# Stick-breaking stage: GpSimd multiplies the first 512 columns of each unit's weights, VectorE the rest

## What is computed

```python
for blk in range(S // SB_BLOCK):                 # 4 blocks of 128 tokens
    z = einsum('bthd,bshd->bhts', q[:, t0:t1], k[:, :t1]) * scale
    before = s_idx < t_idx
    log_beta = log_sigmoid(z)
    log_1m_beta = where(before, log_sigmoid(-z), 0.0)
    tail = cumsum(log_1m_beta, axis=3, reverse=True) - log_1m_beta
    a = where(before, exp(log_beta + tail), 0.0)
    outs.append(einsum('bhts,bshd->bthd', a, v[:, :t1]))
```

## Time and profile before

| | us |
|---|---|
| median of three runs | 2065.1 (2062.42 to 2067.36) |
| profiled execution, whole | 2061.98 |
| its span | 2060.2 |
| TensorE busy | 2018.9 (98%) |
| VectorE busy | 1097.0 (53%) |
| ScalarE busy | 737.7 (36%) |
| GpSimd busy | 227.6 (11%) |

### The profile page before, as it was taken

The page is one execution under the profiler, slowest core; times in us unless marked ns, Lnnn a source line. Parts: engine busy times, 40 slices in busy tenths (PEclk is TensorE's granted clock), DMA queues, the critical chain, the costliest instruction groups (busy, mean ns, idle before and its releaser), DMA issues.

```text
span 2060.2 us, 27336 instructions
## 1 busy us (share of the span) xinstructions
PE 2018.9 (98%) x11013; PEld 1679.3 (82%) x11013; DVE 1097.0 (53%) x1411; ACT 737.7 (36%) x1043; POOL 227.6 (11%) x205
## 2 busy tenths in 40 slices
PE   8999999999999999989999999999999999999998
PEld 7887888888888888868888888888888778888886
DVE  5764765645354453492735445466775435444453
ACT  6444544422122332584412222332673332222221
POOL 4000222300000130002200000322102010000002
PEclk9999999999999999999999999999999999999999
DMA  6231002132222322103222222234213112222221
GB/s 255 82 105 59 23 23 82 62 115 90 102 102 83 121 82 102 42 2 123 82 102 102 82 102 102 103 124 152 82 68 117 62 62 90 95 102 102 94 90 62
DMA packets 28332, 186.91 MB, mean 91 GB/s; under 512 B 3536, under 2 KB 3664, under 8 KB 6480
## 3 DMA queue, kind: packets, MB, share of 16 engines
q1 hardware_dynamic: 25200, 173.48, 23.5%
q0 software_dynamic: 2320, 11.01, 1.5%
q10 hardware_dynamic: 720, 1.11, 0.2%
HBM read 181.39 MB, written 2.10 MB: 89 GB/s over the span
## 4 chain that ended last, share of the span: by engine, by line
PE 90%; DVE 6%; ACT 2%; DMA 1%; issue 1%; POOL 0%; ACTq 0%; DVEq 0%; SPq 0%; POOLq 0%
PE PS L590 88%; DVE Y L2254 1%; DVE KEEP L2638 1%; DVE Y L2638 1%; DVE WL L2254 1%; DMA STG<-weights 1%; DVE Y L2251 1%; ACT WH L1533 1%; DMA MX<-mem_t 0%; PE PS L817 0%; DVE HL L2254 0%; PE PS L619 0%; POOL SQA L474 0%; DVE SQ L2254 0%; ACT SQ L1533 0%
## 5 line engine op out<-in xcount | busy, mean ns | idle before, releaser
L590 PE MATMUL PS<-HH,WH 128*128 128x512 f32 x1544 | 607.6, 394 | 1.0 <-DVE HL L2254 0.8
L590 PE MATMUL PS<-HH,WL 128*128 128x512 f32 x1544 | 601.5, 390 | 0.0
L590 PE MATMUL PS<-HL,WH 128*128 128x512 f32 x1544 | 590.9, 389 | 0.0
L1533 ACT ACTIVATE WH<-STG 128x2048 fp32r<-128x2048 f32 (+2 forms) x168 | 307.2, 1829 | 517.5 <-PE PS L590 516.5
L2254 DVE TENSOR_TENSOR WL<-STG,WH 128x2048 fp32r<-128x2048 f32 (+1 forms) x160 | 358.4, 2240 | 250.1 <-ACT WH L1533 249.9
L590 PEld LDWEIGHTS PS<-HH,WH 128*128 128x128 f32 x1544 | 290.2, 188 | 65.5 <-issue 5.2
L590 PEld LDWEIGHTS PS<-HH,WL 128*128 128x128 f32 x1544 | 290.0, 188 | 60.3
L590 PEld LDWEIGHTS PS<-HL,WH 128*128 128x128 f32 x1544 | 290.2, 188 | 59.9 <-issue 0.7
L590 PE MATMUL PS<-UPH,WH 128*128 128x512 f32 x832 | 324.2, 390 | 1.4 <-DVE UPL L2251 1.4
L590 PE MATMUL PS<-UPH,WL 128*128 128x512 f32 x832 | 323.7, 389 | 0.0
L590 PE MATMUL PS<-UPL,WH 128*128 128x512 f32 x832 | 323.7, 389 | 0.0
(11 more groups left out here) (319 smaller groups left out, 1992.2 us busy)
## 6 DMA issues: line engine op xcount, KB each, us to landing
STG<-weights SPq DMA_DIRECT2D x159, 1024.0 KB, 4.8
KEY_STG<-weights POOLq DMA_DIRECT2D x4, 1024.0 KB, 6.0
XT<-x_t SPq DMA_DIRECT2D x2, 1024.0 KB, 10.3
KEY_X<-mem_t POOLq DMA_DIRECT2D x2, 1024.0 KB, 5.3
out_t<-Y SPq DMA_DIRECT2D x8, 256.0 KB, 2.0
STG<-weights SPq DMA_DIRECT2D x4, 256.0 KB, 6.0
MX<-mem_t ACTq DMA_DIRECT2D x4, 256.0 KB, 7.8
CON<-consts SPq DMA_DIRECT2D x1, 1024.0 KB, 7.1
```

Of the source, the lines that this page charges most:

```text
L590: return pe.matmul(o, l, r, start=start, stop=stop, **kw)
L1533: return act.activation(o, i, f, **kw)
```

## The change

The products of the first 512 columns of all 12 units move from VectorE's stream to GpSimd's. There they stand between the sum of B.in and load_keys(2). They count a new semaphore, sb_wp. TensorE waits for it before the first group of transposes, and ScalarE waits for both before it overwrites KEEP. VectorE keeps the product of columns 512 to 1280.

```diff
@@ gpsimd
             split_lo(R0["B.qk"] + 1)
             sum_squares("B.in")
+            for n in range(12):
+                a, b = SB_PARTS[0]
+                pool.wait_ge(sems["sb_beta"], n + 1)
+                pool.wait_ge(sems["sb_scan"], 4 * n + 2)
+                pool.tensor_tensor(BETA[n % 2][:, a:b], BETA[n % 2][:, a:b], KEEP[n % 2][:, a + 1:b + 1], ALU.mult)\
+                    .then_inc(sems["sb_wp"], 1)
             load_keys(2)
@@ tensor: turn(n)
                     for h in range(2):
-                        pe.wait_ge(sems["sb_w"], 2 * n + h + 1)
+                        pe.wait_ge(sems["sb_w" if h else "sb_wp"], n + 1)
@@ scalar: stick_parts(n)
                 if n >= 2:
-                    act.wait_ge(sems["sb_w"], 2 * n - 2)
+                    act.wait_ge(sems["sb_w"], n - 1)
+                    act.wait_ge(sems["sb_wp"], n - 1)
@@ vector: weights(n)
                     dve.wait_ge(sems["sb_beta"], n + 1)
-                    for h in range(2):
-                        a, b = SB_PARTS[h]
-                        dve.wait_ge(sems["sb_scan"], 4 * n + 2 * h + 2)
-                        tt(BETA[e][:, a:b], BETA[e][:, a:b], KEEP[e][:, a + 1:b + 1], ALU.mult)\
-                            .then_inc(sems["sb_w"], 1)
+                    a, b = SB_PARTS[1]
+                    dve.wait_ge(sems["sb_scan"], 4 * n + 4)
+                    tt(BETA[e][:, a:b], BETA[e][:, a:b], KEEP[e][:, a + 1:b + 1], ALU.mult).then_inc(sems["sb_w"], 1)
```

More of the change, by code:

```diff
@@ L111 @@
 out_ready ow par_in gains_in pool_mm pool_s pool_z qd rcnt_in rk rope_cos rope_done rope_in
-df_b rows_in rows_tr rq rs rsc rv sb_z sb_half sb_keep sb_beta sb_first sb_scan sb_w sb_t sb_at sb_o
+df_b rows_in rows_tr rq rs rsc rv sb_z sb_half sb_keep sb_beta sb_first sb_scan sb_w sb_wp sb_t sb_at sb_o
 lv_t sc_act sc_dve sc_k sc_ws spread sig silu sq sqa sqrt ss st tile t1 gated0 u_mm u_sb uh ul vn vr_mm xf zeroed vrow vtr w_sb
```

## The result

The changed kernel is slower: median 2068.0 us against 2063.0 for the kernel before, run beside it, 20 runs each. The medians differ by 5.0; the ratio is 1.0021 (95% interval 1.0015 to 1.0027), that is +4.3 us (3.1 to 5.6), and the text goes by it. One run of the kernel before took 3417.19 and is no part of the ratio. Forecast was +5.3, slower by over 0.2%, and a median of 2070.5; the kernel before had 2065.1 in its first three runs, from which that was counted, and 2063.0 in all 20.

The account below looks back on a forecast made before the run. VectorE was taken to bound the stick-breaking stage. Added 12.4 less removed 7.1 gave +5.3 us on the median of 2065.1: 2070.4, rounded up to 2070.5; range 2065.5 to 2075.5.

Parts of the forecast that it names:

- VectorE carries the stage, TensorE and ScalarE have room: Stick-breaking stage: VectorE gapless for 56.3 us, 4.63 a unit; TensorE busy 4.18 and ScalarE 4.01 of that.
- Removed, 12 x 0.59 = 7.1: Twelve 512-column products leave VectorE, 0.59 us each, all on the chain: 7.1 us saved.
- Added, 12 x 1.03 = 12.4: Each of twelve GpSimd products costs VectorE 1.03 us through turns over SBUF: 12.4 us, bounds 0 to 15.5.
- The row that gave 1.03: Two VectorE operations with two SBUF inputs took 2.44 us beside one GpSimd product, 1.41 without: 1.03 lost.
- The scan is held like a product: VectorE's scan, reading SBUF twice, was taken to wait for GpSimd as products do; no row showed it.
- Where it lands: GpSimd's turn delays the fourth scan in odd units or the 768-column product in even ones, by about 1.03 us.
- signs of being right: GpSimd rows 1.5 to 2.5, fourth scan or 768-column product about 1.03 longer, VectorE gapless, scan starts 5.07 apart, longer TensorE waits.
- Rival 1: Stage's scans aren't held, so GpSimd works beside them and TensorE's 4.18 a unit binds: -6.0 us, 2059; chance 12%.
- Rival 2: In odd units GpSimd's turn falls on the residue HL<-PS, which isn't held: +2.4 us, 2067.5; chance 8%.
- Rival 3: TensorE's clock gets halved inside the stage, decided at unit four: +8 to +12 us, 2073 to 2077; chance 10%.

Follow-up runs that it names:

- none: The changed kernel without GpSimd's products, so nobody multiplies the first 512 columns: ratio 0.9968 to the kernel before, -6.6 us.
- add_read: The kernel before plus twelve unneeded GpSimd subtractions of 512 columns, one a unit after its second scan: ratio 1.0061 to the kernel before, +12.6 us.
- narrow: The changed kernel with GpSimd multiplying columns 0 to 256 and VectorE 256 to 1280: ratio 1.0028 to the kernel before, +5.8 us.
- third: The changed kernel with GpSimd starting its product after the unit's third scan, not the second: ratio 1.0009 to the kernel before, +1.9 us.
- one_input: The changed kernel with each unit's fourth scan replaced by a maximum of its length reading SBUF once: 0.9967 of the kernel before, -6.8 us.
- add_write: The kernel before plus two unneeded GpSimd memsets of 512 columns a unit, which write SBUF and read nothing: ratio 1.0002 to the kernel before.
- hybrid: The kernel before with GpSimd multiplying the first part only in units 5, 7, 9 and 11, after the third scan: ratio 0.9995, -1.0 us.

## Why the prediction was right

- **VectorE carries the stage, TensorE and ScalarE have room.** Right: VectorE stayed gapless with longer units, and in none the stage shrank by what left VectorE, 5.7, without TensorE in the way.
- **Removed, 12 x 0.59 = 7.1.** Right as a term: none measures -5.7 in the stage, which is 7.1 less the 1.4 below.
- **Added, 12 x 1.03 = 12.4.** The mechanism was right and the size was not: 10.4, at 0.87. What VectorE loses is what is left of GpSimd's operation when the VectorE operation that it met on starting is over, less about 0.05. In even units the third scan ends at 904.26 and GpSimd at 905.18, 0.92 later, with 0.87 lost. In odd units GpSimd is recorded with 1.33 (908.92 to 910.25) and the loss is hardly less, 0.85, because the third scan there is 0.66 long and not 0.39, and ends at 909.36. So the 0.24 more in GpSimd's record is waiting and costs VectorE nothing. The same holds in even units of add_read (1.04 recorded, 0.82 lost) and narrow (0.64 and 0.43). The row that gave 1.03 had a sum of two tiles on GpSimd, 1.29 alone; the product here is 1.09 with about 0.17 of it beside the third scan. Why it is the shorter one wasn't tried.
- **A term left out.** That VectorE keeps the 768-column product was costed at nothing. It now follows the last scan directly and waits for its end, 0.2 in seven units, 1.4. So the stage's sum is 10.4 + 1.4 - 7.1 = +4.7. The two misses, -2.0 and +1.4, partly cancel against the forecast's +5.3; that it came out so close is in part luck. The median of 2070.5 lies 2.5 over the measured 2068.0, of which 2.1 is the median of three runs from which it was counted.
- **The scan is held like a product.** This was carried by a class of operations and no row. It is now shown: the changed kernel and add_read have the fourth scan at its longer time, and add_read changes no wait on VectorE. That it is the second SBUF input that matters is shown for products and residues (third, unit 3: +0.84 with MO, nothing with PSUM); for the scan it is argued from that and from one_input, as no run has a scan with one input outside SBUF. The Trainium skill's rule ("SBUF — State Buffer", "Who interferes with whom") agrees in each point that was run: two SBUF inputs on VectorE, a reading operation on GpSimd (0.87 lost), not a writing one (add_write: 2.96 kept).
- **Where it lands.** The text expected the 768-column product to be held in even units. It was not: GpSimd got its turn ahead of the fourth scan in both kinds of unit. For the sum it made no difference, as the text said. One of its signs of being right failed: GpSimd's rows were to be 1.5 to 2.5 and are 1.09 and 1.33, as GpSimd had only the rest of a narrow scan to wait for (904.09 to 904.26 in even units). Scan starts are 5.00 apart on the mean, where 5.07 was expected.
- **Rival 1** (scans not held) is out by the scans themselves, 3.84 instead of 2.96; one_input's -6.8 is how it would have looked, near the 6.0 worked out for it. **Rival 2** (GpSimd's turn on the residue) did not happen by itself. third makes it happen and gets +1.9 where +2.4 was forecast, but it moves GpSimd's turn in the other units too, so the nearness of the two numbers says little. **Rival 3** (the clock inside the stage) isn't in the changed kernel's profile, 1.00 in every stretch of 10 us from 870 to 930. Four others have a fall at about the place it named. It cost VectorE 0.4 to 0.9 of waiting in third, narrow and hybrid, not 8 to 12, because the clock was back at 1.00 after some 3.4 us.

## What to carry to other kernels

Before GpSimd is given half of an elementwise job, look at what VectorE reads at that time. If VectorE is the bound and its operations have two SBUF inputs, nearly all of GpSimd's working time is paid on VectorE as well, and 512 columns cost 0.87 there where VectorE itself needed 0.59. Beside a VectorE operation that reads PSUM or reads SBUF once, GpSimd's product cost little or nothing, and one semaphore count decided which operation it met: that was 2.4 us of 4.3 here. Even so the best arrangement, hybrid, could not be told from the kernel before.

## What the runs showed of the hardware that was not expected

- When GpSimd waits for a running scan, it goes ahead of VectorE's next such operation, although that follows without a gap: in odd units of the changed kernel GpSimd is recorded with 1.33 instead of 1.09, and it is the fourth scan that is 0.85 longer.
- An operation of VectorE that needs the end of the one before it starts about 0.2 us later than one that doesn't (3.07 against 2.88 from scan start).
- TensorE's clock had a mean of 0.83 over the 10 us from 890 in four of nine profiles (add_read, narrow, third, hybrid), behind the long unit 3 in which TensorE stands still: some 3.4 us at 0.50, the 1.2 GHz level. Hybrid had up to there the very instructions of the kernel before, which kept 1.00. Where it falls changes from one profile to the next: from 820 to 830 us, ahead of all that any edit touches, the mean is 0.83 in five profiles (the changed kernel, add_write, one_input, none, narrow) and 1.00 in the other four. So two profiles can differ by a microsecond or two (3.4 us at half the clock, an estimate of up to 1.7) for no reason in the kernel.
